# One layer of a streaming encoder, one core: the expert sum of a PEER layer with 64 tokens to a slot and every row on TensorE

## What is computed

```python
def peer(n, w_q, keys, u_tab, v_tab):          # per block of 128 tokens
    q = (xb @ w_q).reshape(m, PEER_HEADS, 2, PEER_DKH)
    s = jnp.einsum('nhpc,hpkc->nhpk', q, keys)
    s1, i1 = lax.top_k(s[:, :, 0], 16);  s2, i2 = lax.top_k(s[:, :, 1], 16)
    cand = s1[..., :, None] + s2[..., None, :]
    top, pos = lax.top_k(cand, 16)
    e = i1[pos // 16] * 128 + i2[pos % 16]
    gate = softmax(top)
    act = gelu(einsum('nkd,nd->nk', u_tab[e], xb)) * gate
    return einsum('nk,nkd->nd', act, v_tab[e])
x = x + peer(rmsnorm(x, ln2_g), ...);  y = rmsnorm(x, final_g)
```

## Time and profile before

| | |
|---|---|
| median of 3 runs | 2133.94 us (2130.26 to 2134.75) |
| the profiled execution | span 2123.7 us from the first instruction to the last; its time outside the span is not listed, and the median of the runs is 10.2 us above the span |
| PE matmul busy | 1870.6 us (88% of the span) |
| DVE busy | 1479.7 us (70%) |
| ACT busy | 838.9 us (40%) |
| gathers by POOL | 544, 11.0 us median from issue to landing |
| moved in all | 724.62 MB |

### The profile page before, as it was taken

How to read it: one execution, slowest core, us unless ns; L and a number is a source line. 1 busy time by engine, 2 the same in 40 slices (tenths; PEclk the granted TensorE clock), 3 DMA queues, 4 the chain that set the end, 5 groups by cost and what they waited for, 6 DMA issues and landing times.

```text
span 2123.7 us, 23959 instructions
## 1 busy us (share of the span) xinstructions
PE 1870.6 (88%) x8010; PEld 1214.2 (57%) x8010; DVE 1479.7 (70%) x3271; ACT 838.9 (40%) x2343; POOL 645.4 (30%) x549
## 2 busy tenths in 40 slices
PE   8999999889988899999899779898998877777776
PEld 7888998656555567777566455664454432222321
DVE  4163631398877678789998368898878667667664
ACT  2523111243523476458535134445423333333332
POOL 0000000134332333333434124344433434444442
PEclk9999999899999999999999889999998999999999
DMA  6343225799999999999999989999999999999997
GB/s 230 107 150 129 90 99 180 285 377 354 379 407 378 418 408 368 408 371 370 397 338 386 409 326 375 349 370 370 380 409 418 421 398 421 421 421 421 422 384 302
DMA packets 128132, 724.62 MB, mean 341 GB/s; under 512 B 16336, under 2 KB 23120, under 8 KB 57872
## 3 DMA queue, kind: packets, MB, share of 16 engines
q0 software_dynamic: 78336, 570.46, 67.1%
q1 hardware_dynamic: 49056, 150.49, 19.1%
q10 hardware_dynamic: 624, 2.23, 0.3%
HBM read 714.08 MB, written 8.52 MB: 340 GB/s over the span
## 4 chain that ended last, share of the span: by engine, by line
PE 48%; DMA 25%; DVE 17%; ACT 5%; issue 3%; POOL 1%; DVEq 0%; POOLq 0%; ACTq 0%
DMA arena<-in_uv,arena 18%; PE ps L1068 14%; PE ps L1016 8%; PE ps L738 6%; DVE arena L1938 6%; PE ps L794 5%; DMA arena<-in_stream 3%; PE ps L934 3%; PE ps L885 2%; PE ps L875 2%; PE ps L884 2%; DMA arena<-in_w_q 2%; DMA arena<-in_w_out 2%; DVE arena L1804 1%; POOL arena L1502 1%
## 5 line engine op out<-in xcount | busy, mean ns | idle before, releaser
L1502 POOL DMA_INDIRECT arena<-in_uv,arena x544 | 644.3, 1184 | 1179.8 <-PE ps L1068 783.9
L1068 PE MATMUL ps<-arena 128*128 128x512 f32 (+1 forms) x1660 | 796.6, 617 | 121.2 <-ACT arena L1463 121.0
L1938 DVE CUSTOM_DVE_ANT_0 arena<-arena 128x1024 f32<-128x1024 f32 x544 | 659.6, 1222 | 235.3 <-DMA arena<-in_uv,arena 232.9
L1068 PEld LDWEIGHTS ps<-arena 128*128 128x128 f32 (+1 forms) x1660 | 293.6, 190 | 492.4 <-issue 290.9
L1477 ACT ACTIVATE gelu_d<-dots 128x2 f32<-128x2 f32 x272 | 55.8, 205 | 761.5 <-DVE dots L1938 760.7
L1016 PE MATMUL ps<-arena 128*128 128x294 f32 (+1 forms) x1152 | 291.3, 414 | 14.7 <-DMA arena<-in_stream 9.8
L1016 PEld LDWEIGHTS ps<-arena 128*128 128x128 f32 x1152 | 219.3, 191 | 88.9 <-DMA arena<-in_stream 12.8
L934 PE MATMUL ps<-arena 128*128 128x128 f32 (+1 forms) x1024 | 140.7, 298 | 28.4 <-DMA arena<-in_w_a 13.7
L934 PEld LDWEIGHTS ps<-arena 128*128 128x128 f32 x1024 | 135.8, 206 | 45.8 <-DMA arena<-in_w_a 15.7
L738 PE MATMUL ps<-arena 128*128 128x256 f32 x640 | 141.6, 384 | 3.5 <-DVE arena L1525 3.0
L1463 ACT ACTIVATE arena<-ident,share 128x128 f32<-128x128 f32 x383 | 136.8, 397 | 7.1
(11 more groups left out here) (282 smaller groups left out, 2007.0 us busy)
## 6 DMA issues: line engine op xcount, KB each, us to landing
arena<-in_stream SPq DMA_DIRECT2D x144, 512.0 KB, 5.0
arena<-in_w_a SPq DMA_DIRECT2D x32, 512.0 KB, 8.1
arena<-in_w_out SPq DMA_DIRECT2D x32, 512.0 KB, 10.0
arena<-in_w_q SPq DMA_DIRECT2D x32, 512.0 KB, 7.8
arena<-in_uv,arena POOLq DMA_INDIRECT x544, 11.0
arena<-spill SPq DMA_DIRECT2D x2, 1920.0 KB, 13.9
arena<-in_x_prompt SPq DMA_DIRECT2D x4, 512.0 KB, 5.3
arena<-in_ln_g SPq DMA_DIRECT2D x4, 512.0 KB, 8.8
```

Of the source, the lines that this page charges most:

```text
L1068: mm = pe.matmul(ps[0:L, half, :], diag[on_pe(k) % NDIAG][:, 0:L], ring[k % SLOTS][:, D + half * 512:D + (half + 1) * 512], start=False, s ...
L1502: pool.indirect_dma_start(out=ring[kk % SLOTS], out_offset=None, in_=a["uv"], in_offset=bass.IndirectOffsetOnAxis(ap=idx[:, kk:kk + 1], ax ...
L1938: ins = dve.tensor_tensor_reduce(ring[s][:, 0:D], ring[s][:, 0:D], n2p if t == NTILE else n2[t % 2], 1.0, 0.0, ALU.mult, ALU.add, dots[k / ...
```

## The change

- **Slots.** The partitions of a slot now hold 64 tokens, two experts each: partitions 0 to 63 have an expert of head r, partitions 64 to 127 one of head r + 4, of the same 64 tokens. What was head n of a tile is now pick n = 2 r + g: g is the half of the tile. `tile_order` sets slots of even and odd picks, so of different halves, next to each other, save for the first 8 and last 8 of a tile (tile 0: the first 24 hold 16 of pick 0 and 8 of pick 1, and the last 8 are alone too); the sample's 32 slots stay as they were. There are still 544 slots of 128 rows.
- **Sum.** `diag` is now 128x64 (ACT writes half of it), and its product goes to PSUM partitions 0 to 63 or 64 to 127, by the half. `add_pair(k)` issues both slots of a pair at kk = k + 2: for each half of the 1024, slot k and then slot k + 1. `on_dve`, DVE's `add_row` and `join` are gone: PE adds all 544. `PACE` stays as it is.
- **Tokens.** The dot of a slot needs 64 tokens in both halves of the partitions. `spreads` (SP) copies the normed tile by 4 transfers of 64x1024 (256 KB each) into two buffers, one per half. The copy replaces `n2` being written directly; the transposes read `n2nat`.
- **Scores** are 64x64 parts of the array (two per half of the key and half of the partitions). The first pick of tile 0 needs the queries of heads 0 and 4, so `w_q` comes in the order 0, 4, 1, 2, ... there.
- `picks_at` runs a little earlier; `state_dn` is loaded at slot 260 rather than at the start; `fin` is one buffer; `diag` has 8 buffers.

```diff
@@ order of the slots
+        def tile_order(t):
+            if t == NTILE:
+                return [(n, e) for n in range(SPREAD) for e in range(TOPK)]
+            head = TOPK // 2
+            order = [(0, e) for e in range(head)]
+            if t == 0:
+                order += [(0, e) for e in range(head, TOPK)] + [(1, e) for e in range(head)]
+            for n in range(t == 0, H - 1):
+                for e in range(head):
+                    order += [(n, head + e), (n + 1, e)]
+            return order + [(H - 1, e) for e in range(head, TOPK)]
+        def half_of_tile(k):
+            return pick_of(k) % HALVES
@@ PE
-            def add_row(k):
-                L = rows(k // P)
-                pe.wait_ge(diag_ready, on_pe(k) + 1)
+            def add_pair(k):
+                pe.wait_ge(diag_ready, k + 2)
                 for half in range(2):
-                    mm = pe.matmul(ps[0:L, half, :], diag[on_pe(k) % NDIAG][:, 0:L],
-                                   ring[k % SLOTS][:, D + half * 512:D + (half + 1) * 512], ...)
-                mm.then_inc(slot_free, 1)
+                    for j in (k, k + 1):
+                        t, g = j // P, half_of_tile(j)
+                        m = slice(0, TS) if t == NTILE else slice(g * PAIR, (g + 1) * PAIR)
+                        mm = pe.matmul(ps[m, half, :], diag[j % NDIAG][:, 0:TS if t == NTILE else PAIR],
+                                       ring[j % SLOTS][:, D + half * 512:D + (half + 1) * 512],
+                                       start=False, stop=j == last_of(t, g))
+                        if half:
+                            mm.then_inc(slot_free, 1)
@@ PE, loop over the slots
-                    if not on_dve(k):
-                        add_row(k)
+                    if k % 2 == 0:
+                        add_pair(k)
@@ PE, tile 0
-                    if u == 0 and n == 1:
+                    if u == 0 and n == 2:
                         pe.wait_ge(q0_copied, 1)
@@ SP
+            def spreads():
+                for u in range(NTILE):
+                    yield BT[u] + 21
+                    sp.wait_ge(n2_ready, norms(u) - (u == 3))
...
+                    for g in range(HALVES):
+                        for q in range(HALVES):
+                            sp.dma_start(n2[u % 2][g][q * PAIR:(q + 1) * PAIR, :],
+                                         n2nat[u][g * PAIR:(g + 1) * PAIR, :]).then_inc(spread_in, 16)
@@ DVE
+                elif k % P == 0:
+                    dve.wait_ge(spread_in, (t + 1) * uses(2 * HALVES))
...
-                    for k in (kk - 3, kk - 2):
-                        if on_dve(k):
-                            add_row(k)
```

More of the change, by code:

```diff
@@ L38 @@
 QUARTERS = P // TS
+HALVES = 2
+PAIR = P // HALVES
 SPREAD = H // QUARTERS
@@ L346, in trunk_program @@
         y_ready = sem("y_ready")
[L347 removed]
+        y_out = sem("y_out")
         small_out = sem("small_out")
         block = ctx.enter_context(nc.Block())
[L352 removed]
+        PARAMS = [(ident, "ident"), (upper, "upper"), (lvl, "lvl"), (fold, "fold"), (fold2, "fold2"),
                   (iota16, "iota16"), (dn_w, "dn_conv_w"), (lru_w, "lru_conv_w"),
@@ L475, in freed, with pick_of, column, opens @@
             return conv_ready, CONVS + p - 7 * KC + 1
[L477 to L494, removed]
+        def tile_order(t):
[9 more added lines that the diff above has]
+            return order + [(H - 1, e) for e in range(head, TOPK)]
+        SLOT_OF = [(t * H + n, e) for t in range(NTILE + 1) for n, e in tile_order(t)]
+        def pick_of(k):
+            return SLOT_OF[k][0]
+        def column(k):
+            n, e = SLOT_OF[k]
+            return n * TOPK + e
+        def opens(k):
+            return max(pick_of(j) for j in range(k + 1)) if k >= 0 else -1
+        def half_of_tile(k):
+            return pick_of(k) % HALVES
         def picks_at(kk, part):
             for n in range(LAG, NPICK):
-                first = 12 * (n - LAG) if n < H else TOPK * (n - LAG)
+                if n < H:
+                    first = 13 * n - 17 if n > 1 else 0
+                else:
+                    first = TOPK * (n - LAG) - (TOPK // 2 if n % H and n < NTILE * H else 0)
                 if kk == first + PICK_AT[part]:
@@ L502, in picks_at, with wq_head, wq_last @@
             return []
+        WQ_ORDER = [0, 4, 1, 2, 3, 5, 6, 7]
+        def wq_head(u, i):
+            return WQ_ORDER[i] if u == 0 else i
+        def wq_last(u, lo, hi):
+            return max(i for i in range(KC) if lo <= wq_head(u, i) < hi)
         N_REST = CH_BA - CH_GB
@@ L555, in trunk_program @@
             mine = [("w_a", n, b + n) for n in range(KC)] + [("w_out", k, b + 8 + k) for k in range(KC)]
-            mine += [("g2", u, b + 20)] + [("w_q", n, b + 23 + n) for n in range(KC)] + [("keys", 0, b + 33)]
+            mine += [("g2", u, b + 20)] + [("w_q", wq_head(u, n), b + 23 + n) for n in range(KC)] + [("keys", 0, b + 33)]
             queue += [(c[2], 1, ("tail", u, i), c) for i, c in enumerate(mine)]
@@ L975, in tail @@
                         pe.wait_ge(n2_copied, u + 1)
-                    if u == 0 and n == 1:
+                    if u == 0 and n == 2:
                         pe.wait_ge(q0_copied, 1)
-                        for p in range(2):
-                            rows_p = slice(64 * p, 64 * p + 64)
-                            mm = pe.matmul(ps[:, 2 + 2 * p, 0:P], q[rows_p, 0, 0:P], keys0[rows_p, :],
-                                           start=True, stop=True)
-                        mm.then_inc(s0_done, 1)
-                    product(n, CH_WQ + n, n2t, 5)
+                        scores(0, lambda part, h: keys0[:, part, :]).then_inc(s0_done, 1)
+                    product(wq_head(u, n), CH_WQ + n, n2t, 5)
                 yield b + 33
@@ L989, in tail @@
                 pe.wait_ge(q_copied, 2 * u + len(parts))
-                for p in range(2):
-                    rows_p = slice(64 * p, 64 * p + 64)
-                    for h in range(u == 0, H):
-                        mm = pe.matmul(ps[:, 2 + 2 * p + h // 4, h % 4 * P:(h % 4 + 1) * P], q[rows_p, h, 0:P],
-                                       keys[rows_p, h, :], start=True, stop=True)
+                for n in range(u == 0, H):
+                    mm = scores(n, lambda part, h: keys[:, h, :])
                 if u == 3:
```

145 lines of the change are left out of this document (70 added, 75 removed).

## The result

The changed kernel takes 2218.81 us (median of 4 runs, 2218.33 to 2221.14) against 2132.10 for the kernel before beside it: a ratio of 1.0418 (95% interval 1.0395 to 1.0441). It is slower, by 87 us where 26.5 was forecast; the time lies above the range.

| part, by slots | before | after | difference | forecast |
|---|---|---|---|---|
| before slot 0 | 412.7 | 416.2 | +3.5 | +2.5 |
| delta rules: 0-59, 161-214, 239-333 | 599.9 | 605.4 | +5.5 | -43 |
| tails: 59-95, 214-239, 333-367 | 364.5 | 379.9 | +15.4 | 0, and the copies' 5 |
| second input products: 95-161 | 283.6 | 352.4 | +68.8 | +62 |
| 367 to the end | 463.1 | 463.1 | 0.0 | 0 |

A forecast was written before the change was run, and what follows sets the result against it. Gathers bound the last part, PE 773 to 1007 us, no one engine the delta rules. The terms 59 + 3 - 43 + 0 + 5 + 2.5 = +26.5 us gave 2160.5 us; own range 2135 to 2185, full range 2112 to 2208.

The forecast's parts named there:

- the copies' 5: Token copies of 1 MB each, tile 0's before the gathers, the other three within them: +5 us.
- +59 and +3: Second input products: PE's added slots cost +59 us from 773 to 1007 us and +3 from 723 to 773.
- full overlap of the column halves: On PE, two slots in different column halves run at once, so a pair takes 1.72 us.
- 0.3 us for the changes: Changing the array's parts in and out beside trunk work costs PE 0.31 us, making a pair 2.03 us.
- nothing in the last part: From 1661 to 2030 us the gathers are the bound at 418 GB/s, so time PE or DVE gives back gains nothing.
- The third comes near the floor (24 of 34): Third delta rule part, 1266 to 1543 us: gains 24 of the 34 us possible at 418 GB/s.
- the 43 us: Gain in the three delta rule parts together: 7 of 18, 12 of 17.5 and 24 of 34 us.
- the tails at 0: Parts 584 to 723, 1159 to 1266 and 1543 to 1661 us: no change, bounds -17 and +10 us.
- The clock: A lower granted PE clock could add time, eating into the 43 us outside the last part; no size given.
- Rival 1: Delta rule parts and tails reach the gathers' floor, gaining more than the full part loses: -17 us, 2117 us; chance 0.20.
- the case that the delta parts give nothing: Sign of a wrong forecast: delta rule parts as long as before, putting the time near 2205 us.

The follow-up runs named there:

- Run 2: Changed kernel with PE not adding the rows of slots 95 to 160 (second input products), small stand-in products in their place: 2165.83 us, ratio 1.0147.
- run 1: Kernel before with all 544 rows added by PE in products of 128 columns and none by DVE: 2244.54 us, ratio 1.0525.
- run 5: Changed kernel with PE not adding the rows of slots 2 to 94 and 162 to 366, small stand-in products in their place: 2187.25 us, ratio 1.0266.
- run 3: Changed kernel with one filler product of zero weights per pair on PE beside the delta rules: 2236.50 us, ratio 1.0493.
- run 4: Changed kernel with PE adding slot by slot beside the delta rules, so no two halves run at once there: 2243.72 us, ratio 1.0525.
- run 12: Changed kernel without PE's rows outside the second input products, and with DVE's dots over 512 of 1024 numbers beside the delta rules, no filler: 2155.50 us, ratio 1.0119.
- run 9: Changed kernel without PE's rows outside the second input products, two filler products of zeros per pair beside the delta rules: 2208.69 us, ratio 1.0380.
- run 8: Changed kernel with `PACE` retuned, 87 slots instead of 66 beside the second input products: 2209.75 us, ratio 1.0360.
- run 11: Changed kernel with two pairs added one behind the other at every fourth slot beside the second input products (slots 96 to 159): 2221.98 us, ratio 1.0427.

## Why the prediction was right and wrong

- **Right: what bounds the full part, and the direction.** The forecast's +59 and +3 are +68.8. Run 2 takes 58 of it away, and run 1 shows the same law at full width (93 measured, 61 x 1.72 - 12 by the sum). The sum was low by 7, and by its own terms: for 723 to 773 it counts on half of the 10.7 us that PE is idle, so that 15 - 1.9 - 5.4 = +7.8 and not +3 is left, and for 773 to 1007 it has 2.5 us to spare where the earlier trace rows leave 0.4. With both set right it gives +69. The traces agree: over the whole part PE's idle time fell from 11.2 to 6.9 us, so that idle time took in 4.3 us where the sum had used 12.6 (10.1 and 2.5). A smaller slip is that the DMA engines stand at 9 tenths from the ninth slice on, not the eleventh.
- **Right: full overlap of the column halves, 0.3 us for the changes, and nothing in the last part.** Where a page and a trace could be compared: the Trainium skill's measured 2.38 for three column parts (TensorE: Matmul & The Clock Gate, packing small matmuls) gave an estimate of 2.0 us for a pair before its changes. The trace disagrees with the estimate: four steps of 0.43, no slower than a single slot.
- **Wrong: "The third comes near the floor (24 of 34)", and the 43 us of which it is part.** This term accounts for 48 of the 67 us that the forecast missed. (The 67 are of the spans; the time itself lies 58 us above the forecast.) It measured +5. The step that failed is the inference from the earlier trace rows: a chain that passes through PE for 25 us (1394.94 to 1420.54 us) was taken as proof that PE's slots set the pace of the part. Just ahead of that stretch the same chain runs through DVE's picks and dots, and behind it through a gather:

```profile
1391.12 1.22 DVE arena L1938
...
1394.94 1.13 PE ps L875 x8
...
1420.79 8.79 DMA arena<-in_uv,arena
```

In its place the runs showed that PE's slots as they stood did not set the length of these parts: at full width and at half width the parts take 605 us (run 1), and with no rows at all 593 (run 5). Only more work on PE than that made them longer (runs 3 and 4). Each slot's pair passes from DVE's dot through ACT to PE, and PE's trunk products feed DVE again, all in order on both engines. Shortening PE's share moves the wait to DVE's dots and to the gathers, as the shares of the chain in run 5 show; -12 for PE alone, -23 for DVE alone, -56 for both, each from one profile. What share each has, and whether they hold the parts in turn, stays open (run 12). The forecast looked at loads (DVE 84 to 93%, PE 92 to 93%) and concluded "room"; on two engines that wait on each other such loads left no gain of that size.
- **Wrong: the tails at 0.** They were +15.4, of which 5 had been booked to the copies. In them the rows that had been DVE's went to PE, and the kernel of run 1, with neither copies nor halves, shows +4.2 and +9.4 in the first and third. Run 5, without rows, gives 2.8 and 7.6 back. So in the third it is mostly the rows' move to PE again, and in the first this is 3 to 4 of the 7 us. The rest is unexplained: what the copies cost by themselves was not measured.
- **The clock, an afterthought of the prediction, is a small part at most.** The prediction let it eat into the 43 us. The granted clock did fall by 0.05 to 0.08 in the delta rule parts, where PE's idle time went from 44 to 105 us. The Trainium skill (TensorE: Matmul & The Clock Gate, HAM oscillation) says that PE's waits for data between products can put its clock back to half; the trace agrees with that. The trunk's products covered 10 us more than before and 12 more than in run 1, so this is the most that the clock took. Runs 3 and 9 raised it and paid for the work that did so. Run 5 is the one where it matters: there the trunk's products cover 74 us more than in the changed kernel, so the 12 us it gained say less of what the rows cost at full clock than of what their removal is worth with the clock that comes with it.
- **Rival 1** needed both the floor in all parts and a cheap full part, and had neither. The 0.20 on it was too much, and the range, up to 2208, held the case that the delta parts give nothing, which the text itself put near 2205, but left nothing above it for the tails.

No run beats the kernel before; the nearest that computes everything is run 8, 77 us slower. DVE had the spare time exactly in the part where PE had none, and taking its 61 rows away there is what this change cannot earn back.

## What to carry to other kernels

Doubling an engine's rate on one kind of work pays only where that engine alone is the bound; count how much of that work stands there now, and how much of it someone had moved elsewhere. Here, where two in-order engines hand work to each other and both are at 84 to 93%, relieving one gave a tenth to a fifth of what was taken off it (12 us for 114 less of PE's busy time, 23 for 107 less of DVE's), and both together at least the sum. Cost such an edit by a fraction like that, and test it by taking the work out altogether before building the faster version of it, with an eye on the clock, which may fall with the work. A chain of waits through an engine shows where the time was, not that it would leave with that engine's work.

## What the runs showed of the hardware

- Two float32 products of 128 rows by 64 columns in different column halves, to the same PSUM bank and different partitions, run wholly at once (two records within 0.03 us), and the second half's records start ahead of records of the first half that come earlier in the program. A pair takes 1.94 us as busy time where a pair of one half takes 3.65.
- Going from 128-column parts to 64 and back costs PE 0.34 us (2.06 less the 1.72 of four steps, in the changed kernel; 8 visits fewer and 2.7 us less in run 11).
- In the first delta part of run 12 the DMA engines moved 414 GB/s in all, next to the 418 of the last part, where there is nothing beside the gathers.
- With PE's rows left out, the granted clock of the delta parts fell from 0.92, 0.92 and 0.88 to 0.73, 0.74 and 0.64, and the same trunk products covered 322 us instead of 248 (run 5).
